# High and low products of the gate and up blocks, pair by pair, in a two-layer hybrid decoder

## The reference, cut to what matters

```python
def swiglu(t, w_gate, w_up, w_down):
    return (jax.nn.silu(t @ w_gate) * (t @ w_up)) @ w_down

for l in range(DEPTH):                     # DEPTH = 2, D_MODEL = 1024, D_FF = 2816, SEQ = 256
    x = x + 0.5 * swiglu(rmsnorm(x, ffn1_norm[l]), ffn1_w_gate[l], ffn1_w_up[l], ffn1_w_down[l])
    h = rmsnorm(x, mix_norm[l])
    ...
    x = x + mixed @ w_o[l]
    x = x + 0.5 * swiglu(rmsnorm(x, ffn2_norm[l]), ffn2_w_gate[l], ffn2_w_up[l], ffn2_w_down[l])
```

## Time and profile before

| | before |
|---|---|
| median of 3 runs | 938.1 us (938.1 to 938.32) |
| span of the profiled execution | 935.2 us |
| TensorE matmul busy | 922.3 us, 99% |
| TensorE weight load busy | 784.0 us, 84% |
| VectorE busy | 624.9 us, 67% |
| ScalarE busy | 533.6 us, 57% |
| high products of the blocks (line 1379) | 1280, 391 ns each |
| low products of the blocks (line 1386) | 1280, 283 ns each |
| weights loaded | 304 x 512 KB |

### The profile page before, as it was taken

One profiled execution on the slowest core, in us unless ns is written; L12 is line 12 of the kernel. 1 busy time (PEld: TensorE's weight loads), 2 busy tenths in 40 slices (PEclk: granted clock), 3 DMA queues, 4 the chain that ended last, 5 costly groups with the idle time before them and its releaser, 6 DMA issues.

```text
span 935.2 us, 14752 instructions
## 1 busy us (share of the span) xinstructions
PE 922.3 (99%) x4970; PEld 784.0 (84%) x4970; DVE 624.9 (67%) x937; ACT 533.6 (57%) x1034; POOL 74.6 (8%) x159
## 2 busy tenths in 40 slices
PE   7999999999999999999999999999999999999998
PEld 5888888888788888888888888888887888888887
DVE  5766666685887666666676666666858776666663
ACT  7655554566875555554555555555669565555551
POOL 3000000023320000000020000000342100000000
PEclk9999999999999999999999999999999999999999
DMA  7855555551064755555556555555501566555541
GB/s 290 267 184 191 191 185 196 179 184 65 23 223 156 250 183 190 192 189 193 180 160 239 197 183 189 193 189 175 199 1 65 199 207 207 194 185 193 188 157 46
DMA packets 45814, 165.43 MB, mean 177 GB/s; under 512 B 5296, under 2 KB 5296, under 8 KB 45776
## 3 DMA queue, kind: packets, MB, share of 16 engines
q1 hardware_dynamic: 44496, 160.98, 50.2%
q0 software_dynamic: 992, 3.42, 1.2%
q10 hardware_dynamic: 288, 0.54, 0.1%
HBM read 163.86 MB, written 1.05 MB: 176 GB/s over the span
## 4 chain that ended last, share of the span: by engine, by line
PE 92%; DVE 3%; ACT 2%; issue 1%; DMA 1%; DVEq 1%; POOL 0%; SPq 0%; POOLq 0%
PE UV L1379 31%; PE UV L1386 16%; PE A L1316 12%; PE A L1319 11%; PE A L1320 11%; PE UV L1316 2%; PE UV L1320 2%; PE UV L1319 2%; PE UV L1641 1%; PE UV L1331 1%; ACT work L791 1%; DMA raw<-stream 1%; DVE wlo L905 1%; PE UV L1622 1%; PE A L1608 0%
## 5 line engine op out<-in xcount | busy, mean ns | idle before, releaser
L905 DVE TENSOR_TENSOR wlo<-raw,whi 128x1024 fp32r<-128x1024 f32 x304 | 370.5, 1224 | 127.8 <-ACT whi L555 127.3
L555 ACT ACTIVATE whi<-raw 128x1024 fp32r<-128x1024 f32 x304 | 317.0, 1051 | 11.2 <-DMA raw<-stream 11.0
L1379 PE MATMUL UV<-acts,whi 128*128 128x512 f32 x1280 | 318.8, 391 | 0.0
L1379 PEld LDWEIGHTS UV<-acts,whi 128*128 128x128 f32 x1280 | 234.9, 188 | 46.8 <-DVE wlo L905 1.5
L1386 PEld LDWEIGHTS UV<-acts,wlo 128*128 128x128 f32 x1280 | 174.3, 190 | 12.1
L1386 PE MATMUL UV<-acts,wlo 128*128 128x256 f32 x1280 | 178.8, 283 | 0.0
L1316 PE MATMUL A<-whi,ht_hi 128*128 128x512 f32 x352 | 138.2, 392 | 0.0
L1319 PE MATMUL A<-wlo,ht_hi 128*128 128x512 f32 x352 | 137.9, 392 | 0.0
L1320 PE MATMUL A<-whi,ht_lo 128*128 128x512 f32 x352 | 137.0, 389 | 0.0
L630 ACT ACTIVATE ht_hi<-work 128x256 fp32r<-128x256 f32 x80 | 33.4, 418 | 121.9 <-DVE work L996 121.9
L626 ACT ACTIVATE work<-UV 128x256 f32<-128x256 f32 x80 | 30.7, 384 | 88.8 <-PE UV L1386 88.6
(11 more groups left out here) (217 smaller groups left out, 849.6 us busy)
## 6 DMA issues: line engine op xcount, KB each, us to landing
raw<-stream SPq DMA_DIRECT2D x304, 512.0 KB, 3.3
gain<-norm_gains POOLq DMA_DIRECT2D x5, 512.0 KB, 5.7
out<-x SPq DMA_DIRECT2D x4, 256.0 KB, 2.1
sgain<-small_gains POOLq DMA_DIRECT2D x2, 324.0 KB, 4.1
x<-x_in SPq DMA_DIRECT2D x1, 512.0 KB, 3.6
x<-x_in ACTq DMA_DIRECT2D x1, 512.0 KB, 7.5
cs<-rope POOLq DMA_DIRECT2D x1, 128.0 KB, 5.4
cgain<-col_gains POOLq DMA_DIRECT2D x2, 1.0 KB, 4.2
```

The costliest lines, as they stand in the source:

```text
L555: act.activation(whi_half(unit, half), raw[:, n % RAW, :], ACT.Copy).then_inc(hi_done, 1)
L905: dve.tensor_tensor(wlo_half(unit, half), raw[:, n % RAW, :], whi_half(unit, half).bitcast(F32), ALU.subtract).then_inc(split_done, 1)
L1379: last = pe.matmul(UV[c][:, j, :], whi_half(unit, j)[:, k * P:(k + 1) * P], acts[:, :, k, :], start=k == 0, stop=False, skip_group_check=True)
```

## The change

Two functions take the two halves of `columns` apart, and the half groups call them gate high, up high, gate low, up low. The wait for the up block's weights now stands behind the eight high products of the gate block; the gate block's signal `block_done` stands behind eight of the sixteen low products. This is done in `ffn_step` for both half groups and for the first half group of the last group. Group 1 and the second half group of the last group keep `columns`.

```diff
+            def high_columns(l, f, g, c, j, i=0, freed=0):
+
+                unit = l * LU + FFN_AT[f] + 3 * g + c
+                half_split(unit, j, i)
+                for k in range(KD):
+                    last = pe.matmul(UV[c][:, j, :], whi_half(unit, j)[:, k * P:(k + 1) * P], acts[:, :, k, :],
+                                     start=k == 0, stop=False, skip_group_check=True)
+                    if k == 0 and freed:
+                        last.then_inc(unit_freed, freed)
+
+            def low_columns(l, f, g, c, j):
+
+                unit = l * LU + FFN_AT[f] + 3 * g + c
+                for k in range(KD):
+                    last = pe.matmul(UV[c][:, j, 0:SEQ], wlo_half(unit, j)[:, k * P:(k + 1) * P], act_hi[:, :, k, :],
+                                     start=False, stop=k == KD - 1, skip_group_check=True)
+                last.then_inc(block_done, 1)
+
...
             def ffn_step(l, f, g, i=0):
 
-                columns(l, f, g, 0, 0, i)
-                columns(l, f, g, 0, 1, i)
+                high_columns(l, f, g, 0, 0, i)
+                high_columns(l, f, g, 0, 1, i)
+                low_columns(l, f, g, 0, 0)
+                low_columns(l, f, g, 0, 1)
                 down(l, f, g - 1, 1, 0, i, freed=1)
                 down(l, f, g - 1, 1, 1, i)
-                columns(l, f, g, 1, 0, i, freed=1)
-                columns(l, f, g, 1, 1, i)
+                high_columns(l, f, g, 1, 0, i, freed=1)
+                high_columns(l, f, g, 1, 1, i)
+                low_columns(l, f, g, 1, 0)
+                low_columns(l, f, g, 1, 1)
                 down(l, f, g, 0, 0, i, freed=1)
                 down(l, f, g, 0, 1, i)
...
                 g = NG - 1
-                columns(l, f, g, 0, 0)
-                columns(l, f, g, 0, 1)
+                high_columns(l, f, g, 0, 0)
+                high_columns(l, f, g, 0, 1)
+                low_columns(l, f, g, 0, 0)
+                low_columns(l, f, g, 0, 1)
                 pe.wait_ge(h_w_split, sub_no(l, f, g - 1, 1))
                 columns(l, f, g, 1, 0, freed=1)
                 columns(l, f, g, 1, 1)
```

## The result

| | before | after |
|---|---|---|
| median | 937.2 us (20 runs, 936.88 to 938.62) | 935.87 us (20 runs, 935.65 to 937.0) |
| ratio to before | | 0.9985, 95% interval 0.9979 to 0.9991 |
| span of the profiled execution | 935.2 us | 933.6 us |

The change takes 0.15% off. That is the forecast difference (938.1 to 936.7 is 0.9985 too). The absolute time of 935.87 is not in the stated range: it lies 0.13 under its lower end, 936.0. The kernel before itself has come down, from 938.1 in the three runs that the prediction had to 937.2 over twenty. The interval means 0.8 to 2.0 us less, so the runs alone do not tell the forecast gain of 1.4 from the 1.8 of the larger one; the trace does.

A forecast was written before the change was run, and what follows sets the result against it. The tensor engine's start-to-start matmul spacing was taken as the bound, with no cover over it. One round trip of 0.020 us saved in each of 68 pairs gives 1.4 us: 938.1 - 1.4 = 936.7 us, range 936.0 to 938.4.

The forecast's parts named there:

- the larger gain: Rival for the changed pairs: low run keeps its short first spacing at the blocks' border, 936.3 or less; chance 0.07.
- The sum: Each changed pair takes 5.539 instead of 5.560 us, 0.020 saved, 68 pairs in four stages: 1.4 us.
- The sixteen low products: Price of the doubled low run in each changed pair, not shown by the trace; held to make no difference.
- the charge behind eight: Going from eight low products back to 512-column products costs 0.027 us; assumed the same behind sixteen.
- The case of drained instructions: Rival: sixteen short products drain the tensor engine's ready instructions, restart 0.31 instead of 0.23, 942.1 us; chance 0.05.
- the dearer end of the longer run: Rival: first 512-column spacing behind sixteen low products is 0.25, costing 1.3 us, 938.0; within order worth nothing, chance 0.14.
- the border of the two low blocks: Where the low blocks meet in a pair; keeping the short first spacing there would save 1.8 us in all, 936.3.
- The rule by columns: Contrary rule: matmul gap is N/2.4 + 2.5 ns by columns alone, so block order is worth nothing, 938.1.
- The later signal: Gate block's signal in changed pairs: gate copy 1.8 us later, h about 0.55 later, slack 3.7 us, no wait.
- The walk through the last group's queue: Vector engine's queue in the last group: second pair's h complete at 190.83, 0.33 before needed at 191.16; no stall.
- The level: Absolute time: median 938.1, 2.9 above the profiled span of 935.2, the start and final store in it unchanged.
- gave the measurement 0.2: Measurement was said to move any forecast by about 0.2 us, three runs before lying at 938.1 to 938.32.

The follow-up runs named there:

- Turns of one product: The kernel before with the 68 pairs alternating one high and one low product: 942.23 us, ratio 1.0057.
- last_pair: The changed kernel with the second pair of the last group in the new order too: 938.94 us, ratio 1.002 to before.
- wait_early: The kernel before, old order, with the wait for the second block's weights ahead of the first block in the loop: 937.09 us, ratio 1.0001.
- low_512: The changed kernel with low products of 512 columns instead of 256 in the 68 pairs: 1053.08 us.
- low_128: The changed kernel with low products of 128 columns instead of 256 in the 68 pairs: 930.05 us.
- group_one_too: The changed kernel with the second pair of group 1, ahead of the loop, in the new order too: 935.87 us, ratio 0.9984 to before.

## Why the prediction was right, and where it was not

**The sum.** 5.539 us a pair were forecast and measured, 8.287 a half group, 132.6 for the sixteen of the loop (132.59). 68 x 0.020 = 1.4 us; the medians of twenty runs differ by 1.33. The stage from its first gate block to the end of its last one takes 163.43 instead of 163.75 us in the traces, and the four stages save 0.32 to 0.34 each. Every term came out of start-to-start distances; durations (0.39 and 0.28 us) would have given none of it.

**The sixteen low products.** The unknown was taken at the charge behind eight, 0.027. The trace after has 0.113 at the first spacing, 0.119 to 0.120 at the other fifteen, and 0.027 behind them. The case of drained instructions, 942.1, did not come about, nor did the dearer end of the longer run. The time of 935.87 lies where the prediction put the larger gain, 936.3 or less, but that is the level (below): the border of the two low blocks kept no short spacing, and the pairs gained the 0.020 of the forecast.

**The rule by columns.** The Trainium skill ("TensorE: Matmul & The Clock Gate", Back-to-back issue gap) would have left the time unchanged. The same section of the Trainium skill calls N/2.4 + 2.5 ns the gap of an isolated matmul, and for a stream of weight load and matmul it gives about 131 ns at 512 columns, which is further still from the 227 of these traces. The half group of 8.287 against 8.307 disagrees with a price by columns alone, and so do the table above (a 512-column product costs more or less by what went before) and the spacings, 0.227 and 0.120 where the formula gives 0.216 and 0.109. Turns of one product, 0.57% slower with the same products, show the dependence best.

**The later signal.** Forecast 1.8 us later for the gate copy, 0.55 for h: measured 1.81 and 0.55. The walk through the last group's queue, shifted by the 0.52 us that the kernel after is ahead there, against the trace of the kernel after (DVE, then the product that waits for h):

```profile
181.94 0.42 DVE L987 TENSOR_TENSOR work<-UV,work 128x256 f32<-128x256 f32 x1 [1.58 <-ACT work L618]
...
186.88 0.42 DVE L987 TENSOR_TENSOR work<-UV,work 128x256 f32<-128x256 f32 x1
187.21 1.22 DVE L905 TENSOR_TENSOR wlo<-raw,whi 128x1024 fp32r<-128x1024 f32 x1
188.49 0.43 DVE L991 TENSOR_TENSOR work<-UV,work 128x256 f32<-128x256 f32 x1
...
189.87 0.43 DVE L1001 TENSOR_TENSOR ht_lo<-work,ht_hi 128x256 fp32r<-128x256 f32 x1 [0.49 <-ACT ht_hi L630]
...
190.62 0.39 PE L1316 MATMUL A<-whi,ht_hi 128*128 128x512 f32 x1
```

Forecast: gate sum 182.46, second gate sum 187.38, split 187.73, up sum 189.01. The rows plus 0.52: 182.46, 187.40, 187.73, 189.01. The h is complete at 190.30, the product starts at 190.62, 0.32 of cover as said. last_pair shows that the cover was real and small.

**The level: the step that failed.** The prediction took 935.2 of the span, called the 2.9 up to 938.1 the start and the final store around it, and gave the measurement 0.2. Over the 158 executions with both numbers the device time is 2.07 to 2.24 above the span of the same execution. The profiled execution was thus one of some 937.3, and the few microseconds that the text ahead of the prediction puts around the span are these 2.1; the other 0.8 was no work around the span but other executions that were longer inside it. The 0.2 for measurement failed with it: it was the spread of three runs, and seven of the 82 runs of that kernel lie at 938.1 or above, those three among them. With these terms 937.3 - 1.4 = 935.9 would have been the forecast, and 935.87 was measured. The three runs then lay at the high end of 936.6 to 938.6, in which all 82 runs of that kernel fall, with medians by set of 937.2, 937.0, 937.5 and 937.2.

Where executions may differ, the traces of the kernels suggest. From the start of one marked block to the next, all kernels here that have the same order in a stretch agree to about 0.1 us: the first stage from its first gate block to the end of its last one takes 163.75 in before and in wait_early, and the stretch from there over the whole mixer to the next gate block 111.00 to 111.12 in every kernel but last_pair. The time up to the first gate block does not: 24.67 in before, 24.83 in wait_early, 24.45 after, 24.04 to 24.99 in the others, and 27.07 in low_512, where the clock fell. The scalar engine's second weight split and the first gate block in last_pair and then in low_128:

```profile
7.38 1.06 ACT L555 ACTIVATE whi<-raw 128x1024 fp32r<-128x1024 f32 x1 [0.26 <-DMA raw<-stream]
...
24.04 0.51 PE L1379 MATMUL UV<-acts,whi 128*128 128x512 f32 x1
```

```profile
8.05 1.06 ACT L555 ACTIVATE whi<-raw 128x1024 fp32r<-128x1024 f32 x1 [0.25 <-DMA raw<-stream]
...
24.99 0.50 PE L1379 MATMUL UV<-acts,whi 128*128 128x512 f32 x1
```

Both splits end a wait for the load of a raw buffer; the one starts at 7.38 and its kernel reaches the first block at 24.04, the other at 8.05 and 24.99. The distance between the two is 16.66 to 16.68 us in eleven of the fourteen traces, and in all fourteen the split ends such a wait. In low_128 and group_one_too it is some 0.27 longer, with 0.2 us more of waiting at 16.7 to 16.9 for normalised activations, and in low_512 it is 17.99, at the lower clock. So the first loads' landing and the time up to the first gate block move together, over 0.8 us among the thirteen traces at the full clock. I read this from one trace each of different kernels with the same beginning; no run changed the loads, and no two traces are of one kernel, so that this is also what moves one kernel's executions is argued, not shown. The falling clock is a second, rarer part: of the twenty runs of after the four with a mean clock of 0.998 have a median of 936.47, the other sixteen of 935.84. Of the span's 1.64 us between the two profiles, 1.4 is the pairs and 0.22 is this start (24.67 against 24.45).

## What to carry to other kernels

On a matmul-bound stretch measure start to start, and run by run: the spacing depends on the widths of the products before, so try to keep products of one width together, and measure the whole trip, down and up. Before moving a signal for it, walk the consumers' fixed queues at the end of the loop as well as inside it, for that is where 1.8 us were free in seventeen pairs of a stage and cost 1 us in the eighteenth. A forecast of an absolute time needs the profiled execution's own time, not the median of three others; where only the span is known, the range has to take in the spread of the runs.

## What the runs showed of the hardware

A step back to 512 columns costs 0.111, 0.036, 0.027, 0.040 and 0.000 us behind products of 128, 192, 256, 384 and 512 columns, spread over three (192) to ten (128) products. With the low run's own change of spacing the whole trip costs 0.060, 0.013, 0.020, 0.067 and 0.000 us. Cutting the blocks of the kernel before into turns of four cost 0.023 us a further trip, into turns of one under 0.006. Products of 128 columns were spaced like those of 192, at 0.112 us. A tensor engine that had waited 0.83 us for its operand lost about 0.2 us more in the spacings behind the wait. After a wait of 2.83 us at the start, in one execution, the granted clock was 0.50 for the next thirteen products.
